# Hybrid RWKV-7 and FoX layer: packing of the solved blocks' way back, slots of the inverses and the chain, the order of the value products, and the root of the group norm

## The reference

```python
u = rmsnorm(h, attn_norm_g) @ w_in
y_rwkv = rwkv7_mix(...)      # 16 heads x 64: state update per token, group norm, bonus, gate
y_fox = fox_mix(...)         # 16 heads x 64: causal softmax attention with forget bias
h = h + concat(y_rwkv, y_fox) @ w_out
hn = rmsnorm(h, ffn_norm_g)
h = h + (silu(hn @ w_gate) * (hn @ w_up)) @ w_down
e = rmsnorm(p @ ple_proj, ple_norm_g)
gate = sigmoid(rmsnorm(h, ple_gate_norm_g) @ ple_gate_w + ple_gate_b)
h = h + gate * e
```

## Time and profile before

| | us |
|---|---|
| three runs: median (lowest to highest) | 2901.72 (2898.87 to 2904.9) |
| the profiled execution: its time | 2899.26 |
| its span | 2897.3 |
| PE busy in the span | 2782.7 (96%) |
| DVE, ACT, POOL busy | 1161.8, 1001.3, 216.3 |
| groups and tail, from the first slab of group 0 to the first out slab | about 69 to 1093 |

### The profile page before, as it was taken

How to read it: one execution, slowest core, us unless ns; L and a number is a source line. 1 busy time by engine, 2 the same in 40 slices (tenths; PEclk the granted TensorE clock), 3 DMA queues, 4 the chain that set the end, 5 groups by cost and what they waited for, 6 DMA issues and landing times.

```text
span 2897.3 us, 41123 instructions
## 1 busy us (share of the span) xinstructions
PE 2782.7 (96%) x15562; PEld 2206.9 (76%) x15562; DVE 1161.8 (40%) x1677; ACT 1001.3 (35%) x1388; POOL 216.3 (7%) x343
## 2 busy tenths in 40 slices
PE   7989998998998979999999999999999999999998
PEld 5777676666666747888888888888888888888787
DVE  6643652553453343333333333333333333334544
ACT  5433533433442333343322333223332222233521
POOL 2100110120120011100000000000000000001300
PEclk9999999999999989999999999999999999999999
DMA  4221121112113104222223332233222322223332
GB/s 159 87 67 55 56 78 51 62 51 81 48 60 87 67 30 162 99 102 94 99 83 97 106 100 95 84 97 108 94 94 85 103 101 99 97 82 100 104 123 76
DMA packets 107733, 255.33 MB, mean 88 GB/s; under 512 B 35657, under 2 KB 37193, under 8 KB 107625
## 3 DMA queue, kind: packets, MB, share of 16 engines
q1 hardware_dynamic: 106352, 249.73, 26.9%
q0 software_dynamic: 1280, 4.20, 0.4%
HBM read 244.90 MB, written 8.98 MB: 88 GB/s over the span
## 4 chain that ended last, share of the span: by engine, by line
issue 75%; PE 14%; POOL 3%; DVE 2%; ACT 1%; SPq 0%; DMA 0%; POOLq 0%; DVEq 0%; ACTq 0%
PE bank L288 4%; PE bank L285 4%; PE bank L289 3%; PE bank L320 2%; POOL probs L971 1%; POOL scratch_pool L116 1%; SPq L1187 0%; DVE w_lo L280 0%; PE bank L470 0%; DMA solved_scratch<-solved 0%; POOL acc_e L1740 0%; POOL carried L994 0%; POOL sg_t L963 0%; POOL M_t L980 0%; PE bank L442 0%
## 5 line engine op out<-in xcount | busy, mean ns | idle before, releaser
L280 DVE TENSOR_TENSOR w_lo<-raw,w_hi 128x1024 fp32r<-128x1024 f32 (+1 forms) x476 | 541.8, 1140 | 963.5 <-ACT w_hi L273 953.5
L273 ACT ACTIVATE w_hi<-raw 128x1024 fp32r<-128x1024 f32 (+1 forms) x476 | 468.2, 987 | 1044.5 <-PE bank L289 999.2
L285 PE MATMUL bank<-hn_hi,w_hi 128*128 128x512 f32 x1664 | 648.1, 389 | 0.0
L289 PE MATMUL bank<-hn_hi,w_lo 128*128 128x512 f32 x1664 | 647.3, 389 | 0.0
L288 PE MATMUL bank<-hn_lo,w_hi 128*128 128x512 f32 x1664 | 647.3, 389 | 0.0
L285 PE MATMUL bank<-in_hi,w_hi 128*128 128x512 f32 x1086 | 467.3, 430 | 55.2 <-DMA T_t<-solved_scratch 31.2
L288 PE MATMUL bank<-in_lo,w_hi 128*128 128x512 f32 x1086 | 442.4, 407 | 0.0
L289 PE MATMUL bank<-in_hi,w_lo 128*128 128x512 f32 x1086 | 428.8, 395 | 0.0
L288 PEld LDWEIGHTS bank<-hn_lo,w_hi 128*128 128x128 f32 x1664 | 312.4, 188 | 65.3 <-issue 0.5
L285 PEld LDWEIGHTS bank<-hn_hi,w_hi 128*128 128x128 f32 x1664 | 312.4, 188 | 65.1 <-issue 0.5
L289 PEld LDWEIGHTS bank<-hn_hi,w_lo 128*128 128x128 f32 x1664 | 312.4, 188 | 64.9
(11 more groups left out here) (233 smaller groups left out, 2161.7 us busy)
## 6 DMA issues: line engine op xcount, KB each, us to landing
raw<-w_gu SPq DMA_DIRECT2D x176, 512.0 KB, 3.4
raw<-w_mix SPq DMA_DIRECT2D x136, 512.0 KB, 3.6
raw<-w_down SPq DMA_DIRECT2D x64, 384.0 KB, 3.1
raw<-w_down SPq DMA_DIRECT2D x64, 320.0 KB, 2.8
raw<-ple_gate SPq DMA_DIRECT2D x32, 512.0 KB, 3.5
x_raw<-xT SPq DMA_DIRECT2D x4, 1024.0 KB, 11.6
h_t<-xT SPq DMA_DIRECT2D x4, 1024.0 KB, 8.8
out<-h_t POOLq DMA_DIRECT2D x16, 256.0 KB, 2.3
```

The costliest lines, as they stand in the source:

```text
L273: nc.scalar.activation(w_hi[:, ring_slots(par2, half), 0:cols[half]], raw[:, half, 0:cols[half]], ACT.Copy).then_inc(hi_ready, 1)
L280: nc.vector.tensor_tensor(w_lo[:, s, 0:cols[half]], raw[:, half, 0:cols[half]], w_hi[:, s, 0:cols[half]].bitcast(F32), ALU.subtract).then_ ...
L285: nc.tensor.matmul(out, w_h, x_hi, start=start, stop=False, skip_group_check=True)
L289: return nc.tensor.matmul(out, w_l, x_hi, start=False, stop=stop, skip_group_check=True)
```

## The change

Six things: the solve does two steps in a slot, from slot 19 on; blocks are taken in s 6 right behind the weight loads (ahead of the stores and small loads of that slab) and returned in s 7; the return stores in two transfers and spreads in 8, each of 16 by 32 runs of 64 bytes; the slots of inverses and chain are moved and the chain's pitch is 5 with U two slots behind R0 and the state one slot behind U; the value products of two heads are done at slots 49 and 89, in turn, from two buffers `probs_T`; the group norm's root is Ln and Exp on ACT, without DVE's reciprocal. The clearing of `M_t` on POOL is spread out, half of it in s 6.

```diff
-SOLVE_SLOT = 22
-X_SLOTS, D_SLOTS = (52, 57), (54, 59)
-CHAIN_SLOT, CHAIN_STEP = 62, 4
-U_AT, STATE_AT = 1, 3
+SOLVE_SLOT, SOLVE_RATE = 19, 2
+X_SLOTS, D_SLOTS = (42, 47), (44, 49)
+CHAIN_SLOT, CHAIN_STEP = 52, 5
+U_AT, STATE_AT = 2, 3
...
-    solved_dram = f32("solved_scratch", [P, 2, SB, SB]).ap()
+    solved_dram = f32("solved_scratch", [P // SB, 2, SB, SB, SB]).ap()
...
+    at[0] = overlay + 4 * 4 * SEQ
+    probs_T = [sb("probs_T_even", [P, TT, SEQ])]
     probs = sb("probs", [P, 2, SEQ])
-    probs_T = sb("probs_T", [P, TT, SEQ])
+    probs_T.append(sb("probs_T_odd", [P, TT, SEQ]))
...
-            if j == 0:
+            if j == 1:
                 pe.wait_ge(S("fox_v_tok_ready"), 2 * gp + 2)
                 pe.wait_ge(S("y_rwkv_ready"), 2 * gp + 2)
-            if j == 2:
+            if j == 3:
                 pe.wait_ge(S("o_ready"), 2 * gp + 1)
             for kb in range(TT):
-                last = nc.tensor.matmul(b7[hp(j), kb * P:SEQ], fv_tok[:, kb, j * HD:(j + 1) * HD],
-                                        probs_T[:, kb, kb * P:SEQ], start=kb == 0, stop=kb == TT - 1,
-                                        skip_group_check=True)
-            last.then_inc(S("pv_done"), 1)
+                for head in (j - 1, j):
+                    ins = nc.tensor.matmul(b7[hp(head), kb * P:SEQ], fv_tok[:, kb, head * HD:(head + 1) * HD],
+                                           probs_T[head % 2][:, kb, kb * P:SEQ], start=kb == 0, stop=kb == TT - 1,
+                                           skip_group_check=True)
+                    if kb == TT - 1:
+                        ins.then_inc(S("pv_done"), 1)
...
-                nc.scalar.activation((t1, t2)[ft][:], var_bank[ft][:], ACT.Sqrt, scale=1.0 / HD, bias=cb(CB_GN)
-                                     ).then_inc(S("y_std_ready"), 1)
+                nc.scalar.activation((t1, t2)[ft][:], var_bank[ft][:], ACT.Ln, scale=1.0 / HD, bias=cb(CB_GN)
+                                     ).then_inc(S("y_log_ready"), 1)
+            for ft in range(2):
+                act.wait_ge(S("y_log_ready"), 2 * gp + ft + 1)
+                nc.scalar.activation((t1, t2)[ft][:], (t1, t2)[ft][:], ACT.Exp, scale=-0.5
+                                     ).then_inc(S("y_rstd_ready"), 1)
...
-            if i == 0 and j > 0:
+            if i == 0 and j == 2:
                 act.wait_ge(S("pv_done"), 4 * gp + j)
...
-            dve.wait_ge(S("y_std_ready"), f + 1)
-            nc.vector.reciprocal(rs[:], rs[:]).then_inc(S("y_rstd_ready"), 1)
...
-        j = st - SOLVE_SLOT + 1
-        if 1 <= j < SB - 1:
+        last_step = SOLVE_RATE * (st - SOLVE_SLOT + 1)
+        for j in range(max(1, last_step - SOLVE_RATE + 1), min(last_step, SB - 2) + 1):
...
-        if j == SB - 1:
+        if last_step == SB - 2 + SB % 2:
...
-        if st in (0, 1):
-            if st == 0 and not (isinstance(g, int) and g == 0):
-                pool.wait_ge(S("pv_done"), 4 * g)
-                own_wait(pool, 5)
-            nc.gpsimd.memset((V_t, T_t)[st][:], 0.0).then_inc(S("blocks_cleared"), 1)
+        if st < NC // 2:
+            pool_clear(pool, NC // 2 + st, g)
+        if st in (4, 5):
+            nc.gpsimd.memset((V_t, T_t)[st - 4], 0.0).then_inc(S("blocks_cleared"), 1)
...
-                sp.dma_start(solved_dram, solved[:]).then_inc(S("solved_stored"), 16)
-                sp.wait_ge(S("solved_stored"), 16 * (g + 1))
+                for which in range(2):
+                    sp.dma_start(solved_dram[:, which].rearrange("b i r c -> b i (r c)"),
+                                 solved[:, which].rearrange("p r c -> p (r c)")).then_inc(S("solved_stored"), 16)
+                sp.wait_ge(S("solved_stored"), 32 * (g + 1))
                 for hb in range(P // SB):
                     rows, cols = slice(SB * hb, SB * hb + SB), slice(SB * hb % CH, SB * hb % CH + SB)
-                    for which, t in enumerate((V_t, T_t)):
-                        sp.dma_start(t[rows, :, cols], solved_dram[rows, which].rearrange("i r c -> r i c")
-                                     ).then_inc(S("solved_landed"), 16)
+                    sp.dma_start(VT_t[rows, :, cols], solved_dram[hb].rearrange("w i r c -> r (w i) c")
+                                 ).then_inc(S("solved_landed"), 16)
...
+                    if s == 6:
+                        take_blocks(g)
...
-                        take_blocks(g)
-                    if s == 8:
+                    if s == 7:
                         return_blocks(g)
```

More of the change, by code:

```diff
@@ L216, in layer @@
     after_keys = at[0]
+    at[0] = overlay + 4 * 4 * SEQ
+    probs_T = [sb("probs_T_even", [P, TT, SEQ])]
+    assert at[0] == after_keys
     probs = sb("probs", [P, 2, SEQ])
-    probs_T = sb("probs_T", [P, TT, SEQ])
+    probs_T.append(sb("probs_T_odd", [P, TT, SEQ]))
     at[0] = after_keys
-    V_t = sb("V_t", [P, 2 * NC, CH])
-    levels_at = at[0]
-    T_t = sb("T_t", [P, 2 * NC, CH])
+    VT_t = sb("VT_t", [P, 4 * NC, CH])
+    V_t, T_t = VT_t[:, 0:2 * NC, :], VT_t[:, 2 * NC:4 * NC, :]
+    levels_at = at[0] - 4 * 2 * NC * CH
     blocks_at = at[0]
@@ L417, in pe_finish @@
             else:
-                pe.wait_ge(S("y_std_ready"), 2 * gp + 1)
+                pe.wait_ge(S("y_log_ready"), 2 * gp + 1)
             for k in range(2):
@@ L451, in pe_attention @@
             if q == 0:
-                pe.wait_ge(S("y_std_ready"), 2 * gp + 2)
+                pe.wait_ge(S("y_log_ready"), 2 * gp + 2)
             if q == 1:
@@ L460, in pe_attention @@
         q = attention_item(s, kt, "values")
-        if q is not None and q % TT == TT - 1:
+        if q is not None and q % (2 * TT) == 2 * TT - 1:
             j = q // TT
             pe.wait_ge(S("probs_T_ready"), 16 * gp + q + 1)
-            if j == 0:
+            if j == 1:
                 pe.wait_ge(S("fox_v_tok_ready"), 2 * gp + 2)
                 pe.wait_ge(S("y_rwkv_ready"), 2 * gp + 2)
-            if j == 2:
+            if j == 3:
                 pe.wait_ge(S("o_ready"), 2 * gp + 1)
             for kb in range(TT):
-                last = nc.tensor.matmul(b7[hp(j), kb * P:SEQ], fv_tok[:, kb, j * HD:(j + 1) * HD],
-                                        probs_T[:, kb, kb * P:SEQ], start=kb == 0, stop=kb == TT - 1,
-                                        skip_group_check=True)
-            last.then_inc(S("pv_done"), 1)
+                for head in (j - 1, j):
[4 more added lines that the diff above has]
+                        ins.then_inc(S("pv_done"), 1)
     slot_of = lambda s, kt: KT * (s - 6) + kt
@@ L507, in pe_levels @@
             if m == 0:
-                pe.wait_ge(S("solved_landed"), 256 * (g + 1))
+                pe.wait_ge(S("solved_landed"), 128 * (g + 1))
             else:
@@ L684, in act_attention @@
             act.wait_ge(S("probs_turned"), 16 * gp + q + 1)
-            if i == 0 and j > 0:
+            if i == 0 and j == 2:
                 act.wait_ge(S("pv_done"), 4 * gp + j)
-            nc.scalar.activation(probs_T[:, 0:i + 1, tok(i)],
+            nc.scalar.activation(probs_T[j % 2][:, 0:i + 1, tok(i)],
                                  pt_bank[q % 2][:, 0:n].rearrange("p (k c) -> p k c", c=P), ACT.Copy
@@ L977, in pool_clear @@
             pool.wait_ge(S("R_ready"), 2 * g + 2)
+            own_wait(pool, 4)
+        if c == NC // 2:
             pool.wait_ge(S("c_stored"), 32)
-            own_wait(pool, 4)
+            if not (isinstance(g, int) and g == 0):
+                pool.wait_ge(S("pv_done"), 4 * g)
+            own_wait(pool, 5)
         nc.gpsimd.memset(M_t[:, c], 0.0).then_inc(S("M_cleared"), 1)
@@ L1712, in group @@
                             pool_rwkv_prep(pool, s, kt, g)
-                            if s == 5 and kt >= NC:
-                                pool_clear(pool, kt - NC, g)
+                            if s == 5 and kt in (6, 8, 10, 12):
+                                pool_clear(pool, (kt - 6) // 2, g)
                         else:
```

## The result

The changed kernel takes 2874.62 us (median of four runs, 2873.09 to 2875.82) against 2901.02 (2898.87 to 2904.9) for the kernel before, in the same job: a ratio of 0.9905 with a 95% interval of 0.9893 to 0.9917, so 26.4 us less. Forecast were 43.6 us less and 2856; the range, 2836 to 2880, holds the result. The profiled execution took 2873.09 with a span of 2871.4.

The account below looks back on a forecast made before the run. PE was taken to have work nearly always, so time could come only from its idle stretches, slow stretches and shorter products. 30.0 - 21 + 19.4 + 15.2 = 43.6 us off 2899.3 gave 2856 us, range 2836 to 2880.

Parts of the forecast that it names:

- Part A: Earlier solve and return in eight transfers shorten PE's wait for the inverses' blocks at slot 42: 30.0 us saved, bounds 9 and 36.
- The new cost of a wait: PE at slot 42, per group: 2.5 us wait, 1.0 lower clock, 0.3 starting again, 3.8 against 11.3 before.
- the 2.6: Microseconds from the solved blocks' store to the first spread on SP, second store issue included; between 2.0 and 4.2.
- Part B: The chain's new slots make PE wait for U and the state, 5.3 us a group: 21 us lost, bounds 6 and 30.
- The 0.3 at slot 64: Chunk 2's U at slot 64, its rounding ahead of the state's turn: a wait of 0.3 us a group.
- a rival at 5 us a wait: Four short chain waits a group each lower the clock for 10 us: 80 us lost, 2936 us; chance 0.04.
- signs of being wrong: Blocks' wait staying near 7.8 us, a pair's value products taking 4.6 us, or the clock falling in the chain.
- Part C: Value products of two heads side by side, half of 4.6 us of waits gone, less slot 32's price: 19.4 us saved.
- saved 2.4 x 8 = 19.2: Eight pairs of heads' value products, each taking about 2.4 us side by side instead of 4.8.
- Part D: Group norm's root by Ln and Exp: wait at slot 17 gone, tail's wait 4.2 us shorter; 15.2 us saved, 10 to 18.
- Halves one behind the other: Rival: the two heads' value products do not run side by side; 17.4 us less saved, 2873 us; chance 0.17.
- Costs by runs: Rival: a return transfer costs by its 64-byte runs, 1.0 us an issue, blocks 3.2 us later; 2877 us; chance 0.13.

Follow-up runs that it names:

- run 9: Changed kernel with chain at slot 58, pitch 4, values in four single-head bursts, square root and reciprocals back (only solve, return, inverses' slots changed): 2874.35 us, ratio 0.9904.
- run 1: Changed kernel with only the chain put back: pitch 4, start at slot 58, U one and state three slots behind R0: 2847.83 us, ratio 0.9816.
- run 5: Changed kernel with the value products back in four bursts of one head, slots 29, 49, 69, 89, two buffers kept: 2882.32 us, ratio 0.9932.
- run 6: Kernel before with only Ln and Exp on ACT in place of the square root and DVE's two reciprocals: 2887.64 us, ratio 0.9945.
- run 4: Changed kernel with the return as before: one store instead of two, sixteen transfers of 256 runs instead of eight of 512: 2886.37 us, ratio 0.9947.
- Run 2: run 1 with the inverses also five slots later (47 and 52, 49 and 54): 2836.87 us, ratio 0.9774.
- Runs 7 and 10: 7: changed kernel, transposition one slot later (8, values 10), 2862.38 us, ratio 0.986; 10: the same with values in single-head bursts, 2878.83 us, ratio 0.9919.
- run 8: Run 2 with the inverses one slot earlier (46 and 51, 48 and 53), chain left at 58: 2830.73 us, ratio 0.9761.
- Runs 11 and 12: run 8's inverses and chain at 58, plus transposition at 8 (values 10), 2818.4 us, ratio 0.971; or at 9 (values 11), 2817.67 us, ratio 0.9704.

## Why the prediction was right or wrong

The direction and the parts were right, and the result lies 5 us inside the upper end of the range. The forecast of what is saved was 17 us too high. All four parts came out on the bad side, A and D by less than the runs can tell, so the errors of the parts didn't make up for each other.

| part | forecast | measured by a run | |
|---|---|---|---|
| A, solve, return, slot 42 | 30.0 saved | 28.0 (run 9) | right |
| B, slots of the chain | 21 lost | 26.8 lost (run 1) | 6 more lost |
| C, values in pairs | 19.4 saved | 7.7 saved (run 5), 13.4 by slots | the term that failed |
| D, Ln and Exp | 15.2 saved | 13.8 saved (run 6) | right |
| sum | 43.6 saved | 26.4 saved (the four above add up to 22.7) | 17 short |

- **Part A.** The new cost of a wait was put at 3.8 and is 4.9. Two terms were off against each other: an issue takes 0.50 and not 0.55, and the way from store to spread 3.76 and not 2.6. I put the second store's issue inside the 2.6; run 4 shows 2.7 in the mean for one store alone, so the 2.6 was right for one, and the second costs 0.9 on top (1.75 in group 0). The clock behind the wait took 1.6, near the upper end of my bounds (1.7); I had taken 1.0. Run 2 and the burst of 3.02 in group 0 of run 5 show it to be the clock, which doesn't fall every time.
- **Part B.** The places were right: U at 55 waits 1.74 to 1.84 (forecast 1.9), U at 70 0.92 to 1.00 (1.3), the state at 82 1.62 to 1.64 (1.8). The 0.3 at slot 64 didn't come. I left out two terms. One is starting again: part A has 0.3 for it, part B nothing, and by run 1 it is some 0.4 behind each of the twelve waits. The other is the clock: I made it a rival at 5 us a wait, with 0.04, and nothing in the forecast. It fell behind two of the twelve waits, at 693 and 932 us, and for some 3 us, not 10. So it was neither of the two, though it is one of the signs of being wrong that the prediction names.
- **Part C.** That heads run side by side was right, to the hundredth, and "saved 2.4 x 8 = 19.2" was too. The waits for ACT's copies fell from 4.6 to 0.7, by more than the half that was forecast. The term that failed is "Slot 29 without its burst lets PE reach slot 32 before POOL is ready, which I price at 0.7 in three groups". I looked at one slot behind one of the two bursts that go. PE loses time again ahead of slots 32, 36 and 37 behind slot 29, and of 77, 84 and 87 behind slot 69, 3.0 a group and 8.9 in all instead of 2.1. Runs 7 and 10 show it in part: with one slot more of cover, C gains 3.6 a group instead of some 2.6, and 1.4 us a group of waiting for POOL is left. The other 6 us or so go with stretches of lower clock that run 5 has not. As some of them stand where the change does nothing, I take them for no effect of part C that another kernel could count on; why they fall there is open, and no run tested it.
- **Part D.** The second product of the norm stands 8.73 us behind the start of Ln, where it stood 12.70 behind that of Sqrt: 4.0 earlier, forecast 4.2. The wait at slot 17 is gone, and the tail's fell from 9.58 to 5.33. Run 6 has 4.4 and 4.6 us where the clock had been low behind slot 17 (0.66 and 0.72 over 300 to 305 and 545 to 551) and 2.9 in group 3, where it had not (1.00 over 790 to 796), for a forecast of 3.65 each. The tail is only 2.3 shorter for a wait 4.2 shorter; why is open.
- **The sum.** I added four parts at full clock. The mean clock was 0.985 before, 43 us not granted, and 0.989 after, 31.6: up to 12 of the 26.4 us gained are clock (up to, because some of it isn't granted while PE stands idle). It is in the sum only for the blocks' wait and for slot 17.
- **Rivals.** Halves one behind the other gives 2873, near the result of 2874.6, and is refuted by the starts 0.01 us apart: a right time for a wrong reason. Costs by runs, near it too (2877), is refuted by run 4.

## What to carry to other kernels

When a burst is taken out of a hand-laid schedule, every producer with a fixed distance in slots loses that much cover: go through all waits of the stretch behind it up to the next burst, not only the next one. Moving work to new slots can cost as much as the move brings; here the chain's new slots gave back nearly all of part A, and a chain whose U doesn't come right behind ACT's busy slots (53 and 69) and whose state isn't due at slot 80 took the cost away. The two heads' products, which use opposite column halves, ran side by side only when they alternated in the program.

## What the runs showed of the hardware that was not expected

- Two products over all 128 rows with 64 stationary columns each ran side by side when they alternated (2.37 us a pair), and with only their ends overlapping when not (3.93).
- The same data stored by two transfers instead of one let the first spread go later in all four groups, by 1.75, 0.65, 0.79 and 0.32 us (3.49 to 3.76 against 2.01 to 3.17). One group alone would have misled by a factor of two.
- Issues of 256 and of 512 runs of 64 bytes both stood 0.50 us apart (16 in 7.95 us, 8 in 4.04).
- ACT loads a table of 1.28 us between Ln and Exp, every time in these traces, also when they follow each other directly (288.34).
- The same wait was followed by a granted clock of 1.00 in one place and of half that in another: 1.74 us at slot 55 in group 0 (1.00 over 220.4 to 224.0) and 1.8 in group 2 (0.52 over 694 to 697); 2.63 us at slot 42 of group 0 in run 5 (burst 3.02 us) and 3.08 in the changed kernel (4.52); and in the kernel before 2.65 at slot 17 of group 1 (0.66 over 300 to 305) and 2.64 in group 3 (1.00 over 790 to 796). What decides between them is open.
- Runs 11 and 12 have the least waits and, with run 8, the highest mean clock of a profiled execution: 0.994, 0.993 and 0.993.
